# Mixer attention: values multiplied as rounded products, with the high and low columns of V in one stationary block and the turned weights in two parts

## The reference

```
pc = masked_softmax(sc, cmp_end[None, :] <= t[:, None])
o_cmp = jnp.einsum("bgrsn,bngd->bsgrd", pc.astype(vc.dtype), vc)     # over 15 compressed keys
ss = jnp.einsum("bqgrd,bgqnkd->bgrqnk", qb, kg) * scale
ps = masked_softmax(ss.reshape(...), ms.reshape(...))
o_s = jnp.einsum("bgrqnk,bgqnkd->bqgrd", ps, vg)                     # over selected blocks
sw = jnp.einsum("bqgrd,bkgd->bgrqk", qb, kw) * scale
pw = masked_softmax(sw, mw).astype(vw.dtype)
o_w = jnp.einsum("bgrqk,bkgd->bqgrd", pw, vw)                        # over a window
o = g[..., 0, None] * o_cmp + g[..., 1, None] * o_s + g[..., 2, None] * o_w
mix = jnp.concatenate([y_a, y_b, y_c], axis=-1) @ w_out[l]
```

## Time and profile before

| what | value |
|---|---|
| median of 3 runs | 1870.49 us (1869.71 to 1872.28) |
| profiled execution, its own time | 1868.49 us |
| its span | 1866.7 us |
| granted TensorE clock, mean | 0.996 |
| PE busy | 1830.5 us, 98% of the span |
| DVE busy | 1302.3 us, 70% |
| ACT busy | 1013.4 us, 54% |

### The profile page before, as it was taken

One profiled execution on the slowest core, in us unless ns is written; L12 is line 12 of the kernel. 1 busy time (PEld: TensorE's weight loads), 2 busy tenths in 40 slices (PEclk: granted clock), 3 DMA queues, 4 the chain that ended last, 5 costly groups with the idle time before them and its releaser, 6 DMA issues.

```text
span 1866.7 us, 21829 instructions
## 1 busy us (share of the span) xinstructions
PE 1830.5 (98%) x9112; PEld 1531.4 (82%) x9112; DVE 1302.3 (70%) x1333; ACT 1013.4 (54%) x1083; POOL 107.6 (6%) x101
## 2 busy tenths in 40 slices
PE   7999999999999999999999999999999999999998
PEld 6788888887978888887888888888888888888886
DVE  4579999987779899897554677655465546875544
...
GB/s 341 153 163 265 357 370 356 359 363 224 137 135 225 359 361 346 375 363 226 188 193 167 195 181 106 207 191 176 191 206 190 176 192 203 134 141 211 190 169 57
DMA packets 220170, 426.57 MB, mean 229 GB/s; under 512 B 7560, under 2 KB 28304, under 8 KB 220064
## 3 DMA queue, kind: packets, MB, share of 16 engines
...
## 4 chain that ended last, share of the span: by engine, by line
PE 92%; DVE 4%; ACT 2%; DMA 1%; issue 0%; POOL 0%; DVEq 0%; SPq 0%
PE ps L485 26%; PE ps L477 25%; PE ps L480 25%; DVE Wlo L426 2%; PE ps L596 2%; PE ps L469 1%; PE ps L470 1%; PE ps L2526 1%; PE ps L1306 1%; PE ps L1619 1%; PE ps L576 1%; PE ps L575 1%; PE ps L574 1%; ACT Whi L414 1%; PE ps L2427 1%; PE ps L2022 1%
## 5 line engine op out<-in xcount | busy, mean ns | idle before, releaser
L426 DVE TENSOR_TENSOR Wlo<-raw,Whi 128x2048 fp32r<-128x2048 f32 (+2 forms) x387 | 865.6, 2243 | 409.9 <-ACT Whi L414 409.2
L414 ACT ACTIVATE Whi<-raw 128x2048 fp32r<-128x2048 f32 (+2 forms) x393 | 736.0, 1878 | 474.9 <-PE ps L485 469.7
L485 PE MATMUL ps<-Whi,XTl 128*128 128x512 f32 (+2 forms) x1496 | 549.5, 377 | 0.0
L477 PE MATMUL ps<-Whi,XTh 128*128 128x512 f32 (+2 forms) x1368 | 521.0, 381 | 9.4 <-DVE Wlo L426 8.0
L480 PE MATMUL ps<-Wlo,XTh 128*128 128x512 f32 (+2 forms) x1368 | 514.8, 376 | 0.0
L485 PEld LDWEIGHTS ps<-Whi,XTl 128*128 128x128 f32 x1496 | 280.7, 189 | 50.6
L477 PEld LDWEIGHTS ps<-Whi,XTh 128*128 128x128 f32 x1368 | 258.4, 189 | 57.5 <-DVE Wlo L426 8.0
L480 PEld LDWEIGHTS ps<-Wlo,XTh 128*128 128x128 f32 x1368 | 258.4, 189 | 44.6 <-issue 0.3
L477 PE MATMUL ps<-Whi,hTh 128*128 128x512 f32 x352 | 137.8, 391 | 0.0
L485 PE MATMUL ps<-Whi,hTl 128*128 128x512 f32 x352 | 137.1, 390 | 0.0
L480 PE MATMUL ps<-Wlo,hTh 128*128 128x512 f32 x352 | 137.1, 389 | 0.0
...
## 6 DMA issues: line engine op xcount, KB each, us to landing
...
```

The lines of the kernel that those rows point to most:

```text
L414: act.activation(Whi[:, i % NS, 0:m * n], raw[:, i % NR, 0:m * n], ACT.Copy).then_inc(w_rounded, tick(w_rounded, "rounded", i))
L426: dve.tensor_tensor(Wlo[:, i % NR, 0:m * n], raw[:, i % NR, 0:m * n], h.bitcast(f32), ALU.subtract).then_inc(w_rest, tick(w_rest, "rest", i))
L477: pe.matmul(o, xh(k, t), h[:, q, :], start=k == first, stop=False)
L485: x = pe.matmul(o, xl(k, t), h[:, q, :], start=False, stop=k == end)
```

## The change

The values are multiplied as rounded products. For each key block and group there is a stationary block `vs[k, m, g]` of 128x128 in f32r: its first 64 columns are V rounded, written by ACT, its last 64 are V minus the rounded, written by DVE (`split_v`, 8 pieces of 128x64 on each engine and layer). The turned weights are kept in two parts, `wTh` by ACT and `wTl` by DVE, so each bank of `flip` is read by both engines, one after the other, and is freed by DVE. PE multiplies each stationary block by both parts. The lower 64 partitions of the bank then hold the products with V's high columns and the upper 64 those with its low ones. They are summed when read: ACT copies one half to `OT` (`mo_part`), DVE adds the other half (L2935 of the new kernel) and frees the bank. The compressed part (`vcz`) needs only 64 columns now and goes into the lower partitions, between the first block's two products. DVE takes over the low part of the result for t = 1 from POOL (`rest_o`), and the last sum, `turn_(5)`, stands on DVE between gmlp and conv. The order of the turns on PE is unchanged.

```
@@ -2347,7 +2350,7 @@
             self.hg = area("mx_hg", [128, 2, 2, 16])
             self.hgr = area("mx_hgr", [128, 4, 32])
             self.kc = area("mx_kc", [128, 2, 16, 2], f32r)
-            self.vcz = area("mx_vcz", [128, 8, 128])
+            self.vcz = area("mx_vcz", [128, 8, 64])
             self.gl = area("mx_gl", [128, 2, 24])
             self.nm = area("mx_nm", [128, 2, 8])
             self.sm = area("mx_sm", [128, 2, 8])
@@ -2357,7 +2360,14 @@
             self.qs = at_(f"mx_qs{l}", [128, 2, 4, 256], f32r, gb_o)
             self.zc = at_(f"mx_zc{l}", [128, 2, 258], f32, gb_o + 2048)
             self.yc = at_(f"mx_yc{l}", [128, 2, 256], f32, gb_o + 2048 + 2080)
-            self.wT = at_(f"mx_wT{l}", [128, 16, 128], f32, sh_o)
+            self.wTh = at_(f"mx_wTh{l}", [128, 16, 128], f32r, sh_o)
+            self.wTl = [at_(f"mx_wTl{l}{i}", [128, 16, 128], f32r, (B_o, Y_o)[i]) for i in range(2)]
+            self.vs = {}
+            for k in range(2):
+                for m in range(2):
+                    for g in range(2):
+                        c = 2048 + 256 * g if m else 1792 + 128 * g
+                        self.vs[k, m, g] = at_(f"mx_vs{l}{k}{m}{g}", [128, 128], f32r, big_o + 4 * (2560 * k + c))
             self.w1 = (at_(f"mx_w1k{l}", [128, 16, 128], f32, B_o), at_(f"mx_w1v{l}", [128, 16, 128], f32, Y_o))
             self.S = [at_(f"mx_S{l}{i}", [128, 8, 256], f32, (B_o, Y_o)[i]) for i in range(2)]
             self.OT = self.P[:, :, 1280:1792].rearrange("p t (k n) -> p t k n", k=4)
@@ -2392,10 +2402,6 @@
         pool.wait_ge(*on("gvar", l))
         pool.tensor_tensor(rs[:, :, 1:2], rs[:, :, 0:1], half(2).rearrange("p (a b) -> p a b", b=1), ALU.pow).then_inc(
             pool_done, tick(pool_done, "groot", l))
-        c = cols(4, 4, 1)
-        pool.wait_ge(*on("hi", "mo", l, 1))
-        pool.tensor_tensor(XTl[c], M.OT[:, 1], XTh[c].bitcast(f32), ALU.subtract).then_inc(
-            pool_done, tick(pool_done, "lo", "mo", l, 1))
         pool.wait_ge(*on("lo", "mb", l, 1))
         load_gb(pool, v)
         norm_pool(pool, v)
@@ -2517,18 +2523,23 @@
             g, t = ITEMS[i]
             nbl = 2 * (t + 1)
             b = bank(pe, "mo", l, i)
+
+            def chosen():
+                pe.wait_ge(*on("wcs", l))
+                pe.wait_ge(*on("vcs", l))
+                for r in range(4):
+                    pe.matmul(PS[b][0:64, r * 128:(r + 1) * 128], M.vcz[:, 2 * r + g, :], M.wcT[:, t, :], start=False,
+                              stop=False)
             for rr in heads(t):
-                pe.wait_ge(*on("wts", l, i, rr[0]))
-            w = M.wT[:, 0:4 * nbl, :].rearrange("p (r n) q -> p n r q", n=nbl)
+                pe.wait_ge(*on("lo", "wt", l, i, rr))
+            pe.wait_ge(*on("vs", l))
+            wh, wl = (w[:, 0:4 * nbl, :].rearrange("p (r n) q -> p n r q", n=nbl) for w in (M.wTh, M.wTl[i % 2]))
             for n in range(nbl):
                 m, k = n // (t + 1), n % (t + 1)
-                c = 2176 + 256 * m
-                pe.matmul(PS[b][:, :], P[:, k, c:c + 128], w[:, n], start=n == 0, stop=False)
-            pe.wait_ge(*on("wcs", l))
-            pe.wait_ge(*on("vcs", l))
-            for r in range(4):
-                x = pe.matmul(PS[b][:, r * 128:(r + 1) * 128], M.vcz[:, 2 * r + g, :],
-                              M.wcT[:, t, :], start=False, stop=r == 3)
+                pe.matmul(PS[b][:, :], M.vs[k, m, g][:, :], wh[:, n], start=n == 0, stop=False)
+                if n == 0:
+                    chosen()
+                x = pe.matmul(PS[b][:, :], M.vs[k, m, g][:, :], wl[:, n], start=False, stop=n == nbl - 1)
             x.then_inc(pe_done, tick(pe_done, "mo", l, i))
 
         def turn_(i):
@@ -2673,6 +2684,14 @@
                 act.wait_ge(*on("kTo", l, g))
                 act.activation(M.kh[to, g], M.kh[ps, g].bitcast(f32), ACT.Copy).then_inc(
                     act_done, tick(act_done, "kTs", l))
+
+        def split_v():
+            act.wait_ge(*on("twice", l, 1))
+            for m, c in ((0, 2176), (1, 2432)):
+                for k in range(2):
+                    for g in range(2):
+                        act.activation(M.vs[k, m, g][:, 0:64], P[:, k, c + 64 * g:c + 64 * g + 64], ACT.Copy).then_inc(
+                            act_done, tick(act_done, "vs_hi", l, m, k, g))
 
         def exp_cmp():
             C = M.Sc[:, :, :, 0:15]
@@ -2702,23 +2721,16 @@
 
         def flip(i):
             g, t = ITEMS[i]
-            for rr in heads(t)[1::2]:
-                n = ("wt", l, i, rr)
+            for rr in heads(t):
                 r0 = rr[0] * 4 if t else rr[0] * 2
-                act.wait_ge(*on(*n))
-                act.activation(M.wT[:, r0:r0 + 4, :], turned(n, 4), ACT.Copy).then_inc(
-                    act_done, tick(act_done, "wts", l, i, rr[0]))
-                for r in rr:
-                    point[("wts", l, i, r)] = point[("wts", l, i, rr[0])]
-                free(act_done, *n)
+                split_act(act, ("wt", l, i, rr), M.wTh[:, r0:r0 + 4, :], turned(("wt", l, i, rr), 4))
 
         def values(i):
             g, t = ITEMS[i]
             act.wait_ge(*on("mo", l, i))
-            ps = slice(64 * g, 64 * g + 64)
-            act.activation(M.OT[ps, t, :, :], turned(("mo", l, i), 4)[ps], ACT.Copy).then_inc(
-                act_done, tick(act_done, "mos", l, i))
-            free(act_done, "mo", l, i)
+            ps, other = slice(64 * g, 64 * g + 64), slice(64 - 64 * g, 128 - 64 * g)
+            act.activation(M.OT[ps, t, :, :], turned(("mo", l, i), 4)[other], ACT.Copy).then_inc(
+                act_done, tick(act_done, "mo_part", l, i))
 
         def turn_(i):
             if 0 <= i - 2:
@@ -2758,6 +2770,7 @@
         keys_cmp()
         k_turn()
         gates()
+        split_v()
         for z in run("uv", evac("uv", 768, ACT.Gelu_apprx_tanh)):
             if z == 0:
                 exp_cmp()
@@ -2842,8 +2855,8 @@
             dve.tensor_tensor(M.kc[:, :, :, 1], PS[where[("kc", l)]][:, 0:32].rearrange("p (g n) -> p g n", g=2),
                               M.kc[:, :, :, 0].bitcast(f32), ALU.subtract).then_inc(dve_done, tick(dve_done, "kcl", l))
             b = where[("kc", l)]
-            dve.tensor_tensor(M.vcz[:, :, :].rearrange("p h (a d) -> p h a d", a=2), bc(PS[b][:, 64:65], (0, 8), (0, 2), (1, 64)),
-                              bc(cst[:, C_OWN:C_OWN + 1], (1, 8), (0, 2), (0, 64)), ALU.mult).then_inc(
+            dve.tensor_tensor(M.vcz[:, :, :], bc(PS[b][:, 64:65], (0, 8), (1, 64)),
+                              bc(cst[:, C_OWN:C_OWN + 1], (1, 8), (0, 64)), ALU.mult).then_inc(
                 dve_done, tick(dve_done, "vcs", l))
             free(dve_done, "kc", l)
 
@@ -2910,17 +2923,31 @@
 
         def flip(i):
             g, t = ITEMS[i]
-            for rr in heads(t)[0::2]:
+            for rr in heads(t):
                 n = ("wt", l, i, rr)
                 r0 = rr[0] * 4 if t else rr[0] * 2
-                dve.wait_ge(*on(*n))
-                dve.tensor_copy(M.wT[:, r0:r0 + 4, :], turned(n, 4)).then_inc(
-                    dve_done, tick(dve_done, "wts", l, i, rr[0]))
-                for r in rr:
-                    point[("wts", l, i, r)] = point[("wts", l, i, rr[0])]
-                free(dve_done, *n)
+                split_dve(dve, n, M.wTl[i % 2][:, r0:r0 + 4, :], turned(n, 4), M.wTh[:, r0:r0 + 4, :])
+
+        def values(i):
+            g, t = ITEMS[i]
+            ps = slice(64 * g, 64 * g + 64)
+            dve.wait_ge(*on("mo_part", l, i))
+            dve.tensor_tensor(M.OT[ps, t, :, :], M.OT[ps, t, :, :], turned(("mo", l, i), 4)[ps], ALU.add).then_inc(
+                dve_done, tick(dve_done, "mos", l, i))
+            free(dve_done, "mo", l, i)
+
+        def split_v():
+            for m, c in ((0, 2176), (1, 2432)):
+                for k in range(2):
+                    for g in range(2):
+                        dve.wait_ge(*on("vs_hi", l, m, k, g))
+                        dve.tensor_tensor(M.vs[k, m, g][:, 64:128], P[:, k, c + 64 * g:c + 64 * g + 64],
+                                          M.vs[k, m, g][:, 0:64].bitcast(f32), ALU.subtract).then_inc(
+                            dve_done, tick(dve_done, "vs", l))
 
         def turn_(i):
+            if 0 <= i - 2:
+                values(i - 2)
             if 0 <= i - 1 < 4:
                 flip(i - 1)
             if i < 4:
@@ -2963,12 +2990,19 @@
                 dve.tensor_tensor(P[:, t, 512:768], P[:, t, 512:768], P[:, t, 0:256], ALU.mult).then_inc(
                     dve_done, tick(dve_done, "z", l, t))
 
+        def rest_o(t):
+            c = cols(4, 4, t)
+            dve.wait_ge(*on("hi", "mo", l, t))
+            dve.tensor_tensor(XTl[c], M.OT[:, t], XTh[c].bitcast(f32), ALU.subtract).then_inc(
+                dve_done, tick(dve_done, "lo", "mo", l, t))
+
         def conv():
             dve.memset(M.zc[:, :, 0:2], 0.0).then_inc(dve_done, tick(dve_done))
```

(7 more changed lines are left out.)

## The result

| | before | after |
|---|---|---|
| median, us (runs) | 1872.28 (7) | 1879.86 (7) |
| lowest to highest, us | 1868.86 to 1876.37 | 1877.64 to 1889.38 |
| profiled execution: time, span, us | 1868.49, 1866.7 | 1879.38, 1877.6 |
| mean granted clock | 0.996 | 0.994 |

The ratio is 1.0043, with an interval of 1.0026 to 1.0061: the change costs 8.0 us (4.9 to 11.4). The forecast of 1877.0 (1871.5 to 1883.0) holds the time, and slower was right. The runs before are those beside the new ones.

A forecast was written before the change was run, and what follows sets the result against it. PE, busy 98%, bounds the kernel before, but DVE's longer list was to make it wait: projection 3.2 us late a layer, 6.4 in two, added to 1870.49 gives 1876.9, say 1877.0, range 1871.5 to 1883.0.

The forecast's parts named there:

- Step 1: Turn 1 on DVE: pieces (1.4 us) and low parts delay the exponentials by 1.05; item 1's weights end at 1120.75.
- Step 2: Turn 2: PE's second scores of item 2 wait 2.15 us for the bank of item 0's values, signalled at 1123.65.
- Step 3: DVE then does four low parts (2.4 us) instead of two copies; maxima of item 2 start at 1125.95, 2.85 late.
- Step 4: Turn 3: reciprocal of item 3 at 1143.85; PE waits 1.5 us to turn its weights, then follows DVE's pace.
- Step 5: Turn 4: DVE's last low part is ready at 1152.0, so PE waits 3.05 us for item 3's values.
- Step 6: Item 3's values to output projection: 3.76 us of PE plus 0.55 waiting for a bank; projection starts 1156.3, 3.2 late.
- The walk: Following DVE's and PE's lists through the first layer's turns, 1110 to 1156: projection 3.2 us late; slower by 3.5 to 10: 0.62.
- What PE saved: On PE in the mixer: quicker f32r values and one wait removed, 4.9 us a layer, 9.8 in the program.
- PE's saving reaches the end: Rival: DVE keeps up and PE gets no new wait, 9.8 us less, 1860.7; chance 0.10, in full or good part.
- Late only at the last item: Rival: DVE delays PE only from item 3's values on, 2.6 us less, 1867.9; chance 0.14 with other mixtures.
- No overlap: Rival: DVE's low parts and additions each cost 0.18 us more, 1882.3; chance 0.14 with the other dearer case.
- New products not at 0.23: Rival: PE's new products run like plain f32, 0.43 us each, 1879; chance 0.14 with the other dearer case.

The follow-up runs named there:

- e2_double: The changed kernel with the low-part product of every key block of items 0 to 2 done three times instead of once: 1878.50 us, ratio 1.0047 to before.
- e3_pe_only: The changed kernel's PE products, without the low parts of V and weights or other new DVE work: 1864.23 us, ratio 0.9965 to the kernel before.
- e1_warm: The changed kernel with twelve extra f32r products that nobody reads on PE before item 3's values: 1876.46 us, ratio 1.0027 to the kernel before.
- e5_late_dve: The changed kernel with DVE's unit splits moved between maxima and weights, the last one behind the gated half's low parts: 1865.02 us, ratio 0.9968 to before.

## Why the forecast held, step by step

**The direction and the mechanism were right.** DVE's longer list, walked from 1110 to 1156, became the bound, and PE's saving turned into waits. e2_double and e3_pe_only show both halves of that. The times of after are compared on the clock of before, so 1.28 is taken off.

*Step 1.* Weights of item 1 end: forecast 1120.75, measured 1121.55 - 1.28 = 1120.27. The pieces took 1.09, not 1.4.

*Step 2.* The bank wait: forecast 2.15, measured 1.37. DVE was 0.5 early (1123.19 for 1123.65), and PE later than I had it, since its saving was smaller.

*Step 3.* Maxima of item 2: forecast 1125.95, measured 1125.46. The low parts and the addition were at 0.60 as priced.

*Step 4.* Reciprocal of item 3: forecast 1143.85, measured 1144.63 - 1.28 = 1143.35. The wait at the turning was 0.75 for 1.5, and the heads at DVE's pace cost 0.62 for 0.45.

*Step 5.* The wait for the last low part: forecast 3.05, measured 3.08; the start forecast for 1152.0 was 1151.86. It is the best hit, partly by luck. DVE had been 0.5 early at the end of item 3's weights and lost 0.36 of it again: the unit's split took 2.31, the addition 0.73 and the signal 0.22, for 2.20, 0.60 and 0.10. PE's smaller saving and its shorter waits cancelled in part.

*Step 6 is where a term was mis-sized.* I had 3.76 for the values and the transposes and 0.55 of waiting, 4.3 in all. It took 5.53 and 6.39, with no bank wait. The walk took PE's durations as fixed. But with the wait of 3.1 us the granted clock fell to its lower level. The windows above give for how long: (3 x 0.37 + 4 x 0.15) / 0.5 = 3.4 us in the first layer, all of it under work, and (6 x 0.32 + 6 x 0.24) / 0.5 = 6.7 in the second, 1.4 of it still in the wait. e1_warm prices it at 1.4 and 2.2. The bank wait of 0.55 didn't appear in after, because DVE caught up meanwhile. With PE at full speed the stretch in e1_warm is 4.15, with a gap of 0.2 before the projection, so the 3.76 was too small by 0.2 even without the clock.

**What PE saved** was overrated: 4.9 a layer forecast, 3.6 to 3.8 by e3_pe_only. An f32r product costs the 0.23 of the forecast, so it lies in what stands around it. Item 2's values before the change, from PE's timeline of before:

```profile
1141.70 1.88 PE L2526 MATMUL ps<-mx_wT,mx_P 128*128 128x512 f32 x4
1143.41 1.05 PE L2530 MATMUL ps<-mx_wcT,mx_vcz 128*128 128x128 f32 x8
```

They ended at 1144.31 and so took 2.61; after it is 2.14. That saves 0.47, not 0.72. The eight small products took 0.90 (1143.41 to 1144.31) and now take 1.02 (1143.07 to 1144.09), though their stationary blocks are half as wide. And the first f32r product behind them takes 0.34, and the one ahead of them 0.32, where 0.23 is the pace within a run. I had counted 0.08 for one such change of form an item. There are two, of 0.09 and 0.11, and with the 0.12 of the small products that is the 0.24 by which 2.14 exceeds my 1.90.

The saving didn't show as less busy time either. From the mark to the projection PE is busy 80.61 and 80.62 us before and 80.21 and 80.89 after, but 77.44 and 77.31 in e3_pe_only. What the new products save, the lower clock and the turning drawn out to DVE's pace (2.36 for 1.74) fill up again. Of the 1.2 us by which the page shows PE busier, 1.0 lies ahead of the mark.

**The sum.** 3.2 a layer forecast for the projection's lateness, 4.32 and 5.00 measured. With 1.38 and 2.24 of it for the clock, 2.9 and 2.8 remain. The walk alone would have been 0.3 to 0.4 too high a layer, and the clock turned it into too little: 9.3 in this pair of profiles, 8.0 by the runs, 6.4 forecast.

**The rivals.** *PE's saving reaches the end* (0.10): its condition was that DVE's new work lie inside the waits for exponentials. The lists didn't do that, and e5_late_dve does, with the split in place of the low parts: 6.0 of the 9.8 then arrive, or of the 7.4 that e3_pe_only measures as the saving. *Late only at the last item*: no, all three places were late. *No overlap*: no, low parts start 0.60 apart. *New products not at 0.23*: right in time by accident (1879) and wrong in its reason. They were at 0.43 only where the clock was low, as e1_warm shows. POOL, and waits of PE on the low parts of V, played no part.
